# The first RWKV pair's features moved ahead into projection and attention, and the modulation blocks split four plus five a pair

## The reference, cut to what matters

```python
pr = pr + mu * (shift_centred(pr) - pr)              # all RWKV inputs
r, k, v, wf, wb, af, ab, g = split(pr)
kk = normalise per head(k * kk_weight)
for d in (forward, backward):
    w_log  = -softplus(-(w0[d] + tanh(wd) @ w2[d])) - 0.5
    a      = sigmoid(a0[d] + ad @ a2[d])
    decay  = exp(-exp(w_log));   key = k * (1 + (a - 1) * ka)
    S = S * decay + (S @ -kk) (kk * a)^T + v key^T;   y += S @ r   # scan over tokens
bonus = sum over d of (r . key * rk) * v
```

## Time and profile before

| quantity | value |
|---|---|
| median of 3 runs | 1749.96 us (1747.49 to 1757.27) |
| profiled execution | 1752.18 us |
| its span | 1750.4 us |
| TensorE matmul busy | 1608.0 us, 92% of the span |
| VectorE, ScalarE, GpSimd busy | 707.9, 564.6, 857.5 us |
| mean granted TensorE clock | 0.954 of full speed |

### The profile page before, as it was taken

The page is one execution under the profiler, slowest core; times in us unless marked ns, Lnnn a source line. Parts: engine busy times, 40 slices in busy tenths (PEclk is TensorE's granted clock), DMA queues, the critical chain, the costliest instruction groups (busy, mean ns, idle before and its releaser), DMA issues. The chain is left out here.

```text
span 1750.4 us, 35639 instructions
## 1 busy us (share of the span) xinstructions
PE 1608.0 (92%) x15692; PEld 1326.3 (76%) x15692; DVE 707.9 (40%) x1062; ACT 564.6 (32%) x809; POOL 857.5 (49%) x397
## 2 busy tenths in 40 slices
PE   5899999687888888989999999999989999999996
PEld 3688878566686876868888888888867788888885
DVE  1333246677675754552121212640284521212135
ACT  3423245543434322233232323132222432323230
POOL 1432200197968552437888888744442344444441
PEclk9999899899999999989999999969989799999998
DMA  7321100021312122214444344212221122222221
GB/s 311 125 74 71 58 1 1 1 99 62 126 57 105 52 100 80 73 48 145 146 145 145 143 146 145 90 48 96 96 96 49 48 96 97 96 96 96 96 96 48
DMA packets 23618, 162.17 MB, mean 93 GB/s; under 512 B 2624, under 2 KB 3264, under 8 KB 4800
## 3 DMA queue, kind: packets, MB, share of 16 engines
q1 hardware_dynamic: 21904, 154.09, 24.6%
q10 hardware_dynamic: 1584, 6.13, 0.9%
HBM read 157.71 MB, written 2.10 MB: 91 GB/s over the span
## 5 line engine op out<-in xcount | busy, mean ns | idle before, releaser
L221 POOL TENSOR_TENSOR v<-raw,v 128x1024 fp32r<-128x1024 f32 x160 | 389.6, 2456 | 420.7 <-ACT v L209 396.1
L238 PE MATMUL bank<-hm,v 128*128 128x512 f32 x2112 | 488.3, 393 | 7.4 <-DVE hm L1895 5.1
L238 PEld LDWEIGHTS bank<-hm,v 128*128 128x128 f32 x2112 | 399.4, 190 | 96.8 <-issue 10.4
L238 PE MATMUL bank<-hid,v 128*128 128x512 f32 x1536 | 349.5, 389 | 0.0
L238 PEld LDWEIGHTS bank<-hid,v 128*128 128x128 f32 x1536 | 288.3, 188 | 59.9
L209 ACT ACTIVATE v<-raw 128x2048 fp32r<-128x2048 f32 x77 | 147.5, 1916 | 420.9 <-PE bank L238 420.8
L2026 DVE TENSOR_TENSOR bank<-bank,rl 128x512 f32<-128x512 f32 x64 | 44.8, 700 | 275.1 <-ACT rl L2005 275.1
L221 POOL TENSOR_TENSOR w<-raw,w 128x1024 fp32r<-128x1024 f32 x22 | 54.2, 2485 | 137.0 <-ACT w L209 137.0
L940 POOL TENSOR_TENSOR raw<-raw,cs 128x2048 f32<-128x2048 f32 x24 | 87.0, 3627 | 52.8 <-DVE at L1395 52.8
L511 PE MATMUL bank<-h,w 128*128 128x512 f32 x600 | 109.1, 344 | 0.0
L511 PEld LDWEIGHTS bank<-h,w 128*128 128x128 f32 x600 | 93.7, 191 | 14.4 <-issue 0.3
(11 more groups left out here) (298 smaller groups left out, 2332.6 us busy)
## 6 DMA issues: line engine op xcount, KB each, us to landing
raw<-w_in SPq DMA_DIRECT2D x119, 1024.0 KB, 4.8
mraw<-wm_in SPq DMA_DIRECT2D x16, 1024.0 KB, 4.8
raw<-wm_in SPq DMA_DIRECT2D x3, 1024.0 KB, 16.4
xres<-x_in ACTq DMA_DIRECT2D x1, 2048.0 KB, 9.0
yb<-wm_in SPq DMA_DIRECT2D x2, 1024.0 KB, 19.9
mixed_in<-wm_in SPq DMA_DIRECT2D x2, 1024.0 KB, 23.4
xres<-x_in SPq DMA_DIRECT2D x1, 2048.0 KB, 8.9
out_T<-xres ACTq DMA_DIRECT2D x8, 256.0 KB, 2.0
```

The costliest lines, as they stand in the source:

```text
L221: i = nc.gpsimd.tensor_tensor(W[1][n % 2][:, k:k + 4], raw[n % 2][:, k:k + 4], W[0][n % 2][:, k:k + 4].bitcast(F32), SUB)
L238: last = nc.tensor.matmul(bank(b(s, m), 0, hi - lo), W[w][s][:, k, m * P:(m + 1) * P], H[h][:, k, lo:hi], start=(k == 0 and w == h == 0), ...
```

## The change

Three things move.

1. The low-rank products of pair 0 go on TensorE into block 10 of the projection, after its third channel group; ScalarE takes tanh and the eight sigmoids there, ahead of the last tile's copy. The sigmoids are written over `raw[0]` and `raw[1]`, whose blocks have been split.
2. The rest of pair 0's features go into the attention: the scans cut into eight quarters on VectorE (units 2 to 9), keys, exponentials and reversed values on ScalarE (units 2, 3, 8, 9, 12, 13, 27, 28), everything else on GpSimd. What VectorE did in L1376, L1383 to L1395 and L1403 is done by GpSimd for pair 0.
3. GpSimd then does four modulation blocks in the attention, and five in each pair instead of six.

Buffers are rearranged so that the RWKV tiles exist during attention: probabilities and attention outputs lie in RWKV tiles not yet used, `Rp` and `Z` lie in the attention's input buffer later.

```diff
 # projection
+                            if n == S_MOD - 1 and k == 2:
+                                lora_pieces()
...
+                def lora_pieces():
+                    pe.wait_ge(later_in, 16 * PAIRS)
+                    pe.wait_ge(tile_free[(S_MOD - 2) % 2][1], nth(S_MOD - 2))
+                    pe.wait_ge(tanh_ready, 1)
+                    for i, (kind, seg, d) in enumerate(PIECES):
+                        if i == 3:
+                            pe.wait_ge(knormed, PAIRS)
+                        if i == 4:
+                            pe.wait_ge(mixed, 14)
+                        if i == NP - 1:
+                            pe.wait_ge(sig_ready, 1)
+                        lo, hi = SEG[seg]
+                        r = slice(d * HD, (d + 1) * HD)
+                        nc.tensor.matmul(bank(LORA_BANK[i], 0, hi - lo), lw[r, 0, kind, :], lora[r, kind, lo:hi],
+                                         start=True, stop=True).then_inc(lora_done, 1)
...
+                def gates():
+                    act.wait_ge(mixed, 13)
+                    nc.scalar.activation(lora[:, 0, :], lora[:, 0, :], ACT.Tanh).then_inc(tanh_ready, 1)
+                    for s in range(2):
+                        act.wait_ge(split_ready[(S_MOD - 1 - s) % 2], nth(S_MOD - 1 - s))
+                    for i, (kind, seg, d) in enumerate(PIECES):
+                        lo, hi = SEG[seg]
+                        act.wait_ge(lora_done, i + 1)
+                        o = sigma[kind][:, d, lo:hi]
+                        nc.scalar.activation(o[:, ::-1] if d else o, bank(LORA_BANK[i], 0, hi - lo), ACT.Sigmoid,
+                                             bias=R("a0" if kind else "w0", 4 * d, 4 * d + 1)).then_inc(sig_ready, 1)
+                        if t == 20:
+                            gates()
 # attention
+            @block.sync
+            def _(sp):
+                sp.wait_ge(kp_ready, 1)
+                sp.wait_ge(bb_ready, 1)
+                sp_load(sp, S_MOD)
+                sp.wait_ge(cum_ready, 2)
+                sp_load(sp, S_MOD + 1)
+                for b in range(AHEAD):
+                    sp_next(sp, S_MOD + b)
+            @block.gpsimd
+            def _(pool):
+                nc.gpsimd.memset(Pp[:].rearrange("p d n j -> p (d n) j")[:, :, 0:1], 1.0)
+                pool.wait_ge(kp_ready, 1)
...             # KTL * k (3 instructions), sigma * kk into BT (3), key sum into bs (1)
+                pool.wait_ge(decay_ready, 4)
+                pool.wait_ge(ksum_ready, 1)
+                nc.gpsimd.tensor_tensor(KTL[:], KTL[:], Pn[:], MUL).then_inc(prod_ready, 1)
+                pool.wait_ge(bb_ready, 1)
+                nc.gpsimd.tensor_tensor(BT[:], BT[:], Pn[:], MUL).then_inc(prod_ready, 1)
...             # PC copy, AT_ (3 instructions), RT (2)
+                for b in range(AHEAD):
+                    mod_block(pool, S_MOD + b, b)
+                def first_pair(u):          # ScalarE, after transposed(u - 1)
+                    if u in (2, 3):
+                        d = u - 2
+                        act.wait_ge(ones_ready, 1)
+                        i = nc.scalar.activation(KTL[:, d], sigma[1][:, d], ACT.Identity, scale=R("ka", 0, 1),
+                                                 bias=oka[:, 0:1])
+                        if d:
+                            i.then_inc(kp_ready, 1)
...             # u = 8, 12: Pp; u = 9, 13: Pn; u = 27, 28: reversed values into Pn
-                nc.scalar.activation(lora[:, 0, :], lora[:, 0, :], ACT.Tanh)
+                def decay_sums(i):          # VectorE, end of turns 2 to 9
+                    d, n = i // 4, N // 4
+                    lo = (i % 4) * n
+                    j = nc.vector.tensor_tensor_scan(AT_[:, d, lo:lo + n], K("scan", lo, lo + n),
+                                                     sigma[0][:, d, lo:lo + n], 0.0, MUL, ADD)
+                    if i % 4 == 3:
+                        j.then_inc(cum_ready, 1)
 # RWKV
             for p in range(PAIRS):
-                key_products(p)
+                if p:
+                    key_products(p)
                 pool.wait_ge(at_ready, p + 1)
                 if p:
                     pool.wait_ge(mod_done, p)
-                for t in range(TURNS):
-                    modulation(S_MOD + TURNS * p + t, t)
+                for b in range(max(MOD_AT[p], AHEAD), MOD_AT[p + 1]):
+                    mod_block(pool, S_MOD + b, b - MOD_AT[p])
...
-            for i in range(NP):
-                lora_piece(0, i)
...
-            for i in range(NP):
-                gate(0, i)
-            keys(0)
-            exponentials(0, 0)
-            exponentials(0, 1)
-            reversed_values(0)
...
-            cumulate(0, 0)
-            cumulate(0, 1)
-            features(0)
-            receptance(0)
+            nc.vector.scalar_tensor_tensor(bs[:], bs[:], R("rk", 0, 1), rT[:, 0, :], MUL, MUL).then_inc(bs_ready, 1)
```

More of the change, by code:

```diff
@@ L459, in build @@
     neg_sink = small[:, 32:40]
+    NCH = N // Q
+    GL = GD - GC
+    AHEAD = 4
+    TURNS = (S_OUT - S_MOD - AHEAD) // PAIRS
+    MOD_AT = [0] + [AHEAD + TURNS * (p + 1) for p in range(PAIRS)]
+    LVL = 5
+    STEPS = NCH - 2
+    PIECES = [(kind, seg, d) for kind in range(2) for seg in range(2) for d in range(2)]
+    SEG = ((0, C), (C, N))
+    NP = len(PIECES)
+    LORA_BANK = (1, 2, 3, 4, 5, 6, 7, 1)
+    sigma = [raw[kind][:].rearrange("p k m -> p (k m)")[:, 0:2 * N].rearrange("p (d n) -> p d n", d=2) for kind in range(2)]
@@ new lines, in mod_block @@
+    def mod_block(pool, n, t):
+        r = raw[n % 2]
+        b = n - S_MOD
+        pool.wait_ge(raw_loaded[n % 2], 16 * (n // 2 + 1))
+        nc.gpsimd.tensor_tensor(r[:], r[:], cs[:, :, 0].unsqueeze(2).to_broadcast([P, KT, 256]), MUL)\
+            .then_inc(mprod_ready, 1)
+        for i, w in enumerate((4, 2)):
+            pool.wait_ge(mprod_ready, 3 * b + i + 1)
+            nc.gpsimd.tensor_tensor(r[:, 0:w, :], r[:, 0:w, :], r[:, w:2 * w, :], ADD).then_inc(mprod_ready, 1)
+        pool.wait_ge(mprod_ready, 3 * b + 3)
+        nc.gpsimd.tensor_tensor(msum[:, t, :], r[:, 0, :], r[:, 1, :], ADD).then_inc(mod_used[n % 2], 1)
@@ L460, in build, with in_order @@
+    def in_order(d, ap):
+        return ((ap[:, 0:N], 0, N),) if d == 0 else ((ap[:, 0:C][:, ::-1], 0, C), (ap[:, C:N][:, ::-1], C, N))
     Q_AT, K_AT, SUM_AT, INV_AT = S_IN + 2, S_IN + 5, S_IN + 7, (S_IN + 8, S_IN + 9)
@@ L488, in _ @@
                     sp.dma_start(lw[:, i], A["lw"][i]).then_inc(later_in, 16)
-                with sp.Fori(0, (NB - 1) // 2) as turn:
+                with sp.Fori(0, (NB - 3) // 2) as turn:
                     up = 2 * turn
@@ L671, in build @@
     NQ = T // P
-    with ExitStack() as st:
-        pr = [sb(st, f"prob{i}", [P, 5 * P]) for i in range(2)]
-        pt = [sb(st, f"probT{i}", [P, 5 * P]) for i in range(2)]
-        oS = sb(st, "oS", [P, PAIRS, NQ, P])
+    rw_sb = ExitStack()
+    AT_, BT, KTL = (sb(rw_sb, n, [P, 2, N]) for n in ("at", "bt", "kt"))
+    RT = sb(rw_sb, "rt", [P, 2, T])
+    Pp = sb(rw_sb, "Pp", [P, 2, NCH, Q + 1])
+    Pn = sb(rw_sb, "Pn", [P, 2, N])
+    bs = sb(rw_sb, "bs", [P, T])
+    oka = sb(rw_sb, "oka", [P, PAIRS])
+    PC = sb(rw_sb, "PC", [P, 3, 2 * NCH])
+    AM = sb(rw_sb, "AM", [P, 2, GD, 2, 2, Q])
+    btt, ktt, vtt = (sb(rw_sb, n, [P, 2, GD, P]) for n in ("b_tok", "k_tok", "v_tok"))
+    XM = sb(rw_sb, "XM", [P, 2, 2, GD, 2, Q])
+    XT, MT = XM[:, 0], XM[:, 1]
+    RKT = sb(rw_sb, "RKT", [P, 2, GL, 2, Q])
+    Rp = att_buf[:, 0:2 * T].rearrange("p (d t) -> p d t", d=2)
+    Z = att_buf[:, NCSA:NCSA + 2 * STEPS * Q].rearrange("p (d s j) -> p d s j", d=2, j=Q)
+    msum = sb(rw_sb, "msum", [P, AHEAD + TURNS, 256])
+    with ExitStack() as st:
+        shared = AM[:].rearrange("p d g h w j -> p (d g h w j)")
+        pr = [shared[:, i * 5 * P:(i + 1) * 5 * P] for i in range(2)]
+        pt = [shared[:, (2 + i) * 5 * P:(3 + i) * 5 * P] for i in range(2)]
+        oS = XM[:].rearrange("p a d g h j -> p (a d g h j)")[:, 0:PAIRS * NQ * P].rearrange("p (a b c) -> p a b c",
+                                                                                          b=NQ, c=P)
         mx, nmx, rs, es, den = (sb(st, n, [P, 4]) for n in ("mx", "nmx", "rs", "es", "den"))
@@ L926, in _ @@
         def _(sp):
-            for n in range(S_MOD, S_OUT):
+            for n in range(S_MOD + AHEAD, S_OUT):
                 sp_next(sp, n)
@@ L930, in _ @@
             sp.dma_start(x[:], A["x"]).then_inc(x_back, 16)
-            sp.dma_start(g2[:], A["g2"]).then_inc(g2_in, 16)
+            sp.dma_start(g2, A["g2"]).then_inc(g2_in, 16)
         @block.gpsimd
         def _(pool):
[L935 to L946, removed]
             def key_products(p):
@@ L976, in lora_piece @@
                 r = slice(d * HD, (d + 1) * HD)
-                if p and i:
+                if i:
                     pe.wait_ge(sig_ready, NP * p + i)
```

(11 more changed lines are left out.)

117 lines of the change are left out of this document (63 added, 54 removed).

## The result

The changed kernel takes 1800.66 us (median of 4 runs, 1795.25 to 1802.53) against 1753.62 of the kernel before on the same chip: a ratio of 1.027, with a 95% interval of 1.022 to 1.031. The forecast was 1730 in a range of 1719 to 1744. The profiled execution took 1800.24 us with a span of 1798.4, its mean granted TensorE clock is 0.92 where it was 0.954.

What follows compares the result with a forecast made beforehand. It attacked the 20.32 us between attention and pair 0, where TensorE waits for VectorE's decayed keys. Terms -20.3 - 2.0 - 4.0 + 3.0 + 3.0 = -20.3 gave 1731.9 from 1752.18, 1730 for the median; range 1719 to 1744.

Steps and rivals of the forecast that it cites:

- Attention: +3 us: Attention: VectorE's denominator sum may wait for GpSimd's running instruction, mostly hidden; 0 to 6 us, taken as 3.
- The low-rank products, +3.0: Projection, block 10: eight low-rank products on TensorE, 2.85 us in a row, with TensorE hardly waiting; +3.0 us.
- The stage: Between attention and pair 0: TensorE's first transpose follows the block's entry directly, so the stage goes; -20.3 us.
- The head: Start of pair 0: TensorE's first four items keep full speed coming from the attention; -2.0 us, bounds 0 and 3.5.
- The scans: Pair 0's inverse: VectorE's scans meet GpSimd at another point, likely its shorter sums; -4 us, bounds 0 and 7.
- bound 0: Pair 0's scans: the low end of the gain, where a scan hits GpSimd's long instruction again; 0 us.
- Rival A: Attention: the scaled maximum L815 waits for GpSimd as well as the sum; 17 us lost, result 1744; chance 0.14.
- Rival B: Attention: all four small VectorE operations wait, a unit takes a whole modulation block; 32 us lost, 1763; chance 0.05.
- Rival C: Start of pair 0: GpSimd is late and TensorE still waits, 16 us less 8 of cover; 1738; chance 0.07.
- the cover that was forecast: End of attention: GpSimd finishes its work there eight us before the attention ends; past that each us counts fully.

Runs made afterwards that it cites:

- e7_den_again: The changed kernel with the denominator's one-column sum written as TENSOR_SCALAR with a pointer operand, run again: 1728.28 us (4 runs), ratio 0.987 to the kernel before.
- e1_den: The changed kernel with the denominator's one-column sum written as TENSOR_SCALAR with a pointer operand, first runs: 1731.3 us (2 runs), ratio 0.987 to the kernel before.
- e3_both: The changed kernel with the denominator's sum as TENSOR_SCALAR and GpSimd's key products held back until the quarter scans are done: 1733.16 us (4 runs), ratio 0.988.
- e8_gate: e7_den_again plus GpSimd's last modulation block in pairs 0 to 2 held until both scans of the next pair are done: 1734.91 us (9 runs), ratio 0.989.
- e9_fill: The changed kernel with two extra 256-column constant matmuls on TensorE in each of attention turns 4 to 8: 1734.45 us (9 runs), ratio 0.992.
- 1: Experiment group: the changed kernel with only the denominator's one-column sum rewritten as TENSOR_SCALAR, run twice: 1731.3 and 1728.28 us.
- 3: Experiment group: the kernel before, GpSimd idle, with one or two scratch scans on VectorE in attention turns 4, 5 and 6: 1753.01 and 1819.23 us.
- 4: Experiment group: the changed kernel with extra constant matmuls on TensorE, in attention turn 23 (1786.74 us) or in turns 4 to 8 (1734.45 us).
- The burst: The changed kernel with five extra 512-column constant matmuls on TensorE in attention turn 23: 1786.74 us (2 runs), ratio 1.020 to the kernel before.
- e5_idle_twice: The kernel before with two 768-column scratch scans on VectorE in each of attention turns 4, 5 and 6: 1819.23 us (2 runs), ratio 1.039.
- e2_late: The changed kernel with GpSimd's key products held back until the eight quarter scans are done: 1769.62, 1765.28, 1764.34 and 1737.2 us, no ratio given.
- e4_before_idle: The kernel before with one 768-column scratch scan on VectorE in each of attention turns 4, 5 and 6: 1753.01 us (8 runs), ratio 1.000.

## Why the prediction was wrong

Stretches of the profiled executions, by TensorE's own markers (the query rotation's first product L540/L603 in the projection, first score, first transpose of pair 0, first level, first result), as differences from the kernel before:

| stretch | forecast | e7_den_again | the changed kernel |
|---|---|---|---|
| up to the rotation product (varies by run) | 0 | -2.6 | +3.4 |
| rest of the projection, with the low-rank products | +3.0 | +4.4 | +3.9 |
| attention | +3.0 | +0.3 | **+66.2** |
| stage between attention and pair 0 | -20.3 | -20.3 | -20.3 |
| head of pair 0 | -2.0 | -2.5 | -2.4 |
| scans in pair 0's inverse | -4.0 | -2.2 | -2.4 |
| the rest | 0 | -2.5 | -0.4 |
| sum | -20.3 | -25.5 | +48.0 |

The attention's +0.3 is the good case: e1_den, the same kernel, has +2.0, and so have e3_both and e8_gate. They start it at a mean clock below 1 (0.79 over the first 8 us of e3_both, 1.00 in e7_den_again), as the changed kernel does; that is about 1.7 of its 66.2 us.

*The step that failed is "Attention: +3 us".* Its mechanism was right: a one-column sum of two SBUF operands waits for the end of GpSimd's running instruction (1.71 us at 259.13, up to 3.38 later). The rule of the Trainium skill that stood behind it (SBUF — State Buffer, Who interferes with whom) holds down to one column here. The direct price was of the right size, rather too high: the two waits ahead of the fall cost TensorE 0.67 + 1.17 = 1.84 us, to which the waits of the scans contribute, and e9_fill shows 0.7 us for the later ones. (The forecast put 1.3 us on an average wait beside GpSimd; the 15 sums of e9_fill from 287 to 328 us take 0.84 on average, 0.69 more than alone.) What failed is the step from VectorE's lateness to the time: 16 x 0.4 = 6 us at worst, taken as 3, which prices only the time that TensorE stands still. Two short gaps, in a stage that otherwise keeps TensorE fed, took the granted clock to 0.50 for 132 us, and the attention took 66.2 us more. Shown by 1 (no wait of the sum, no gap, no fall) and 3 (a gap without GpSimd: the fall); 4 agrees (waits with TensorE kept fed: no fall; a dense stretch: return). The range allowed nothing of the kind: all rivals for the attention priced waits, none the clock, although the forecast itself counted on "clock 1.00" behind the attention in the term for pair 0's head, and the earlier trace rows show transposes and products at almost half speed after gaps of 17.47 and 4.46 us.

*The low-rank products, +3.0,* came to +3.9. They take 3.74 us in place of 2.85, because the last of them waits for the first sigmoid (its `sig_ready`), and that one stands behind a table load which starts only after the first product; TensorE and ScalarE in the projection's last block of the changed kernel:

```profile
230.54 3.74 PE L576 MATMUL bank<-mixed_in,lw 64*128 64x256 f32 x16
```

```profile
231.34 1.28 ACT L648 ACT_TABLE_LOAD   x1 [1.75 <-PE bank L576]
232.63 3.89 ACT L648 ACTIVATE raw<-bank,prm 128x256 f32<-128x256 f32 x8
```

That this is the reason is argued from these rows and the waits in the code; it wasn't tried alone.

*The stage* went whole: TensorE's first transpose is its first instruction of the stage, at 406.09. *The head* was forecast for the reason that TensorE keeps its speed, and in e7_den_again that is so: the first four items take 3.19 us for 5.46, 2.3 of the 2.5. In the changed kernel the -2.4 is in part luck: coming from 0.50, the four items take 4.52 us and give only 0.9; the rest is that TensorE waits less for VectorE's L1528 (L1417 before), 0.20 us for 1.47. *The scans* gave 2.2 to 2.4 and not 4, and not where the forecast looked: the second one met GpSimd again (5.00 us against 5.07), the forecast's "bound 0", and what was won lies at the first, 3.10 us in e7_den_again for 4.98 before, behind which TensorE's gap of 1.57 us is gone. The gate shows that another 4.2 us were there to be had.

*Rival A* (L815 waits as well) is disproved: L979, the same instruction, takes 213 to 216 ns in all 32 units of the changed kernel, beside GpSimd or not, as it did before (214 on average). The widening of L2096 doesn't carry over to one column. *Rival B* would have needed all four small operations to wait; only the sum did, while the reciprocal takes at most 166 ns and the output's scaling at most 285 in all 32 units. That B alone had forecast a slower kernel (1763) doesn't make it right. *Rival C* (GpSimd late) didn't come about: in e7_den_again its last block in the attention ends at 324.6 us, 8 us ahead of the end of TensorE's last attention transposes (332.8), the cover that was forecast.

With the sum's form changed, the kernel takes 1728 to 1731 us, where 1730 was forecast. That is partly luck: in e7_den_again the projection is 1.4 us worse and the scans 1.8 us worse than their terms, while the attention is 2.7 better (its forecast +3 was for the wait that is gone), and 5.1 us lie in the two rows for which nothing was forecast. No other version has a lower median; it is 1.3% under the kernel before.

## What to carry to other kernels

Where a stage keeps TensorE fed with small matmuls, ask of each added wait not only how long TensorE stands but what granted clock the stage keeps afterwards: gaps of 0.67 and 1.17 us cost 66 us here, gaps of 0.41 and 0.73 us nothing. A one-column operation with two SBUF operands beside GpSimd is such a wait; written with one operand as a per-partition scalar it wasn't here. And a forecast that counts on full clock behind a stage should ask what could end it inside the stage. Read the clock by windows before anything else when a stage grows and "busy" doesn't change.

## What the runs showed of the hardware

- The granted clock stayed at 0.50 for 132 us with TensorE fed in 131.62 of them, and 6.98 us of 512-column matmuls brought it back to 1.00 for the same work behind them. The Trainium skill (TensorE: Matmul & The Clock Gate, Part 1) has it that the throttled state is the default and activity releases it. The burst agrees. The 132 us of the changed kernel don't, if activity is read off the profile's busy time: TensorE was fed in nearly all of them and the clock stayed at 0.50.
- A TENSOR_TENSOR of 128x1 with two SBUF operands took up to 3.38 us beside GpSimd (0.13 to 0.15 alone). The same sum as a TENSOR_SCALAR with one operand as a per-partition scalar took 180 to 207 ns in all 32 units of e7_den_again.
- The granted clock fell to 0.50 behind a single gap of 1.40 us in e5_idle_twice, and behind one of 1.34 us, 9 us after one of 0.36, in e2_late. In the changed kernel it fell behind gaps of 0.67 and 1.17 us. It stayed at 1.00 behind gaps of 0.41 and 0.73 us (e4_before_idle) and behind one of 0.70 us (e9_fill).
